# A causal convolution of 31 taps: the first 12 taps of two of its four channel tiles go to ScalarE and GpSimd

## The chip, the core and the metric

The kernel runs on one core of a Trainium2 chip. The time is that of the whole kernel on the device, in microseconds (us), as a median of several runs; lower is better. One further execution was taken with the hardware profiler, and all rows below are from it. Engines are named as the profile does: PE (TensorE), DVE (VectorE), ACT (ScalarE), POOL (GpSimd), SP (SyncE). "L1546" is line 1546 of the kernel before.

## The reference, cut to what matters

Two transformer blocks run over 256 tokens of width 1024. The second one starts with a mixer that has a convolution and a retention half. Only the convolution is touched:

```
def conv_module(a, b, conv_w, conv_b, ln_w, ln_b):
    u = a * jax.nn.sigmoid(b)
    y = lax.conv_general_dilated(
        u, conv_w[:, None, :], window_strides=(1,), padding=[(CONV_WIDTH - 1, 0)],
        dimension_numbers=("NWC", "WIO", "NWC"), feature_group_count=CONV_CH) + conv_b
    yf = y.astype(jnp.float32)
    mu = jnp.mean(yf, axis=-1, keepdims=True)
    var = jnp.mean(jnp.square(yf - mu), axis=-1, keepdims=True)
    yn = (yf - mu) * lax.rsqrt(var + EPS) * ln_w + ln_b
    return jax.nn.silu(yn)
```

CONV_WIDTH is 31 and CONV_CH is 512, so each of 512 channels is filtered by its own 31 weights along the tokens. With channels on the partitions that is 4 tiles of 128 channels x 256 tokens with 31 taps each: 124 multiply-adds of a whole 128x256 tile.

## The kernel before, in words

Each weight matrix streams through a ring of four buffers, `raw`. SP starts the load of a chunk (128x1024 for the phases here) when the chunk four before it has been used up, ACT rounds it to `whi` (split_hi, L365), DVE subtracts to get the rest, `wlo` (split_lo, L376), and PE multiplies with both (L398 to L400, 24 matmuls to a strip). The five engines run programs of their own, each in the order written, and meet only at semaphores.

The stage around the change is `mixb`, with the phase `memk` behind it: 28 steps q = 0 to 27, one weight chunk each, from about 582 to 685 us of the span. Steps 0 to 7 give the four tiles of the gated input `glu`, steps 8 to 11 the queries and keys `qr` that are rotated at once, 12 to 15 the values, 16 to 19 a gate, and 20 to 27 the keys of a memory attention, whose results ACT copies to `km[:, 0]` to `km[:, 7]`. PE, ACT and DVE each have one function that loops over q (pe_mixb, act_mixb, dve_mixb). In a step DVE reads a result out of a bank (L1632), does its share of the rotation (steps 10 to 13, tile e = q - 10: L1569, L1570 and L1572) or of the retention (from step 13, RET0), then split_lo, and then a number of convolution taps: conv_taps, from step 4 (TAP0), as many as the list in taps_before says. A tap is one multiply-add of a 128x256 tile of `glu`, shifted by j tokens, onto `cy` (L1546; the first of a tile, with the bias, is L1542). Tiles 0 and 1 are done first, in turns, then tiles 2 and 3. After step 26 the sums for the layer norm of the convolution follow (dve_layer_norm, from L1590).

PE depends on DVE and ACT at these places, apart from `wlo`: the rotation matmul of tile e at step 9 + e (L1357) needs, for e = 2 and 3, that DVE has read out the one two tiles earlier (L1570, through `rot_step`); the spread of `m_inv` at step 15 (L420) needs DVE's reciprocal of step 14 (L1575); the transposes of the values (L1366, four of them at steps 13 to 16) need ACT's two scaled copies of the one before (L1464, through `rv_copied`); the retention's second product (L1413, at steps 15, 17, 19, 21) needs DVE's masked scores `amat` (L1647) and, from the second on, ACT's root (L1520, through `gn_sd`).

ACT's step is, in order: split_hi, one scaled tile of `mem` (L1452, steps 10 to 17), sigmoids, the scaled copies L1464 (steps 14 to 17), roots and copies of the retention (L1520, L1527 and L1528), and last the copy of the step's bank (act_mixb_copy, L1492; steps 8 to 15 and 20 to 27). POOL has little to do: it computes the rotary angles of the positions near the start of the kernel (L2095 to L2108), fills masks, and in this stage starts loads: `mem_rows`, `mem` and, at steps 5 to 12, four pieces of `decay` (L2143). DVE needs piece u at step 14 + 2u.

Of the kernel before, what the change touches and what calls it, by code (L numbers as in the profile page):

```python
# [26 lines left out]
ALU = mybir.AluOpType  # L27
ACT = mybir.ActivationFunctionType
# [6 lines left out]
NX = 256  # L35
# [8 lines left out]
HEADS = 8  # L44
# [6 lines left out]
TAPS = 31  # L51
# [47 lines left out]
def build(nc, io):  # L99
# [12 lines left out]
    with ctx:  # L112
        def sem(name):
            return ctx.enter_context(nc.semaphore(name))
# [29 lines left out]
        vecs = place("vecs", [P, V_COLS])  # L144
        convw = place("convw", [P, 4 * TAPS])
# [143 lines left out]
        decay_in, mem_in, glu_zero = sem("decay_in"), sem("mem_in"), sem("glu_zero")  # L289
        cs_act, cs_dve = sem("cs_act"), sem("cs_dve")  # L290
        cb_sig, glu_done, conv_step = sem("cb_sig"), sem("glu_done"), sem("conv_step")
        rot_mm, rot_step, rg_done = sem("rot_mm"), sem("rot_step"), sem("rg_done")
        m_scaled, m_hi, m_lo, m_sq, rows_in, m_sd, m_inv, m_bc, m_r = (
            sem(s) for s in ("m_scaled", "m_hi", "m_lo", "m_sq", "rows_in", "m_sd", "m_inv", "m_bc", "m_r"))
# [1015 lines left out]
        sc, sgrp = first["mixb"]  # L1310
        STEPS = counts["mixb"] + counts["memk"]
        TAP0 = 4
        RET0 = 13
        ROWS0, MEM0 = 4, 10
        LN0 = 27

        def taps_before(q):

            steps = [4] * 6 + [3] * 4 + [5] * 3 + [8] * 3 + [7] * 7
            return min(sum(steps[:q - TAP0]), 4 * TAPS)  # L1320

        assert taps_before(LN0) == 4 * TAPS
        RV = 12

        def pe_mixb(pe):
# [106 lines left out]
        def act_mixb(act):  # L1432
            for q in range(STEPS):
                if q < 20:
                    split_hi(act, sc, 1, q, LEAD)
                if q == 0:
                    act_norm(act, N_MIXB, False)
                if q == 1:

                    act.wait_ge(angle_step, ANGLE_STEPS)  # L1440
                    nc.scalar.activation(sinv[:, :], angle[:, :], ACT.Sin).then_inc(cs_act, 1)
                    nc.scalar.activation(cosv[:, :], angle[:, :], ACT.Sin, scale=0.5).then_inc(cs_act, 1)
                if q in (ROWS0, ROWS0 + 1):
                    b = q - ROWS0
                    act.wait_ge(rows_in, 16)
                    nc.scalar.activation(vmem[:, b, :], vmem[:, b, :], ACT.Square,
                                         accum_out=msum[:, b:b + 1]).then_inc(m_sq, 1)
                if MEM0 <= q < MEM0 + KT:
                    e = q - MEM0
                    if e == 0:  # L1450
                        act.wait_ge(mem_in, 16)
                    nc.scalar.activation(mem[:, e, :], mem[:, e, :], ACT.Copy, scale=gain(N_MEM, e)).then_inc(m_scaled, 1)  # L1452
                if q < 8 and q % 2 == 0:
                    act.wait_ge(acc_free, sgrp + q + 1)
                    nc.scalar.activation(sg[:, 0:NX], tg[:, 0:NX], ACT.Sigmoid).then_inc(cb_sig, 1)
                if q == 13:
                    act.wait_ge(m_sq, 2)
                    nc.scalar.activation(col_root[:, 0, 0:2], msum[:, :], ACT.Sqrt, bias=epsc[:, 0:1],
                                         scale=1.0 / D).then_inc(m_sd, 1)
                if RV + 2 <= q < RV + 6:  # L1460
                    t = q - 2 - RV
                    act.wait_ge(rv_tr, t + 1)
                    for b in range(2):
                        nc.scalar.activation(v2[:, b, t * P:(t + 1) * P], ps[3][:, NX + b * P:NX + (b + 1) * P],  # L1464
                                             ACT.Copy, scale=inv[:, b:b + 1]).then_inc(rv_copied, 1)
                if q == 15:
                    act.wait_ge(m_bc, 1)
                    nc.scalar.activation(memr[:, :], ps[7][:, 0:NX], ACT.Copy).then_inc(m_r, 1)
                if 17 <= q < 21:
                    act.wait_ge(acc_free, sgrp + q)  # L1470
                    src = tg if q % 2 else tu
                    nc.scalar.activation(rg[:, q - 17, :], src[:, 0:NX], ACT.Silu).then_inc(rg_done, 1)
                if q >= RET0:
                    act_retention(act, q - RET0)
                act_layer_norm(act, q - LN0)
                if 8 <= q < RV:
                    act_mixb_copy(act, q, qr[:, q - 8, :])
                if RV <= q < RV + 4:
                    if q == RV + 1:
                        act.wait_ge(glu_done, 4)  # L1480
                    if q >= RV + 2:
                        act.wait_ge(rv_tr, q - RV - 1)
                    act_mixb_copy(act, q, (tu if q % 2 else tg)[:, 0:NX])
                if q >= 20:
                    act_mixb_copy(act, q, km[:, q - 20, :])
                    split_hi(act, sc, 1, q, LEAD)

        def act_mixb_copy(act, q, dst):

            act.wait_ge(pe_done, sc + q + 1)  # L1490
            act.wait_ge(acc_free, sgrp + q)
            nc.scalar.activation(dst, ps[banks[sgrp + q]][:, 0:NX], ACT.Copy).then_inc(acc_free, 1)  # L1492

        def act_layer_norm(act, step):
            if step == 1:
# [37 lines left out]

        def conv_taps(dve, a, b):

            for n in range(a, min(b, 4 * TAPS)):
                t, j = n // (2 * TAPS) * 2 + n % 2, n % (2 * TAPS) // 2
                src = glu[:, t, j:j + NX]
                w = convw[:, t * TAPS + j:t * TAPS + j + 1]
                if j == 0:  # L1540
                    dve.wait_ge(glu_done, t + 1)
                    nc.vector.tensor_scalar(cy[:, t, :], src, w, vecs[:, V_CONVB + t:V_CONVB + t + 1], ALU.mult,  # L1542
                                            ALU.add).then_inc(conv_step, 1)
                else:
                    dve.wait_ge(conv_step, n - 1)
                    nc.vector.scalar_tensor_tensor(cy[:, t, :], src, w, cy[:, t, :], ALU.mult, ALU.add).then_inc(conv_step, 1)  # L1546
# [39 lines left out]
        def dve_layer_norm(dve, step):  # L1586
            if step == -1:

                dve.wait_ge(conv_step, 4 * TAPS)
                nc.vector.tensor_tensor(csq[:, 0:2, :], cy[:, 0:2, :], cy[:, 2:4, :], ALU.add).then_inc(ln_sum, 1)  # L1590
                dve.wait_ge(ln_sum, 1)
                nc.vector.tensor_tensor(csq[:, 0, :], csq[:, 0, :], csq[:, 1, :], ALU.add).then_inc(ln_sum, 1)
            if step == 1:
                dve.wait_ge(ln_mu, 1)
                for t in (0, 2):
                    nc.vector.scalar_tensor_tensor(cy[:, t:t + 2, :],
                                                   ps[4][:, 0:NX].unsqueeze(1).to_broadcast([P, 2, NX]), -1.0 / CONV,
                                                   cy[:, t:t + 2, :], ALU.mult, ALU.add).then_inc(ln_cen, 1)
            if step == 2:
                dve.wait_ge(ln_sq, 2)  # L1600
                nc.vector.tensor_tensor(csq[:, 0:2, :], csq[:, 0:2, :], csq[:, 2:4, :], ALU.add).then_inc(ln_sum, 1)
                dve.wait_ge(ln_sum, 3)
                nc.vector.tensor_tensor(csq[:, 0, :], csq[:, 0, :], csq[:, 1, :], ALU.add).then_inc(ln_sum, 1)
            if step == 3:
                dve.wait_ge(ln_sd, 1)
                nc.vector.reciprocal(csq[:, 1, :], csq[:, 1, :]).then_inc(ln_r, 1)
            if step == 4:
                dve.wait_ge(ln_r, 1)
                for t in range(4):
                    nc.vector.scalar_tensor_tensor(cy[:, t, :], cy[:, t, :], vecs[:, V_LNW + t:V_LNW + t + 1],  # L1610
                                                   csq[:, 1, :], ALU.mult, ALU.mult).then_inc(ln_n, 1)
                for t in range(4):
                    dve.wait_ge(c_hi, t + 1)
                    nc.vector.tensor_tensor(oz2[:, 4 + t, 1, :], cy[:, t, :], oz2[:, 4 + t, 0, :],
                                            ALU.subtract).then_inc(c_lo, 1)
# [456 lines left out]
        def _(pool):  # L2072
# [63 lines left out]
            pool.dma_start(vmem[:, :, :], io["mem_rows"]).then_inc(rows_in, 16)  # L2136
            pool.wait_ge(pe_done, sc + 3)
            pool.dma_start(mem[:, :, :], io["mem"]).then_inc(mem_in, 16)
            for u in range(HEADS // 2):
                pool.wait_ge(pe_done, sc + 6 + 2 * u)  # L2140
                if u:
                    pool.wait_ge(decay_in, 16 * u)
                pool.dma_start(decay[:, 2 * u:2 * u + 2, :], io["decay"][:, 2 * u:2 * u + 2, :]).then_inc(decay_in, 16)  # L2143

        @block.scalar
        def _(act):
# [243 lines left out]
```

## Time and profile before

| | before |
|---|---|
| median of 3 runs | 985.16 us (984.95 to 985.96) |
| the profiled execution, its own time | 985.93 us |
| its span, first to last instruction | 984.1 us |
| PE busy | 969.7 us, 99% |
| DVE busy | 693.9 us, 71% |
| ACT busy | 513.3 us, 52% |
| POOL busy | 37.4 us, 4% |
| mean granted clock of PE, share of full speed | 0.997 |

Shares of busy time are averages over the whole span. In a timeline row the first number is the start in us, the second how long the instruction or the run of xN instructions lasted; instructions overlap at their ends, so the rate of an engine is read from start to start. In brackets stands how long the engine was idle before it and what ended that.

### The profile page before, as it was taken

What the parts mean: (1) busy time and instruction counts of PE and PEld (TensorE: products, weight loads), DVE (VectorE), ACT (ScalarE), POOL (GpSimd) and SP (SyncE); (2) the same over time, 40 slices, a digit from 0 to 9 for tenths busy, and PEclk for the clock granted to TensorE, in tenths of its full rate; (3) what the DMA queues carried; (4) which work ended last, traced back from release to release, by engine and by line L of the source; (5) the groups of instructions that cost most, each with busy time, mean ns of one, the idle gap of its engine ahead of it and who ended that gap; (6) DMA issues with size and microseconds to landing.
All of it is one profiled execution on the core that took longest, in us unless ns stands there. A gap on an engine that the chain in (4) does not pass through costs nothing.

```text
span 984.1 us, 19828 instructions
## 1 busy us (share of the span) xinstructions
PE 969.7 (99%) x7333; PEld 919.7 (93%) x7333; DVE 693.9 (71%) x1231; ACT 513.3 (52%) x825; POOL 37.4 (4%) x59
## 2 busy tenths in 40 slices
PE   8999999999999999999999999999999999999997
PEld 7999999999988898999998899888998999998886
DVE  6866675556688778866676559999885398885553
ACT  6544454455465665655454447642765465444441
POOL 4600000001000000000000000000000000000000
PEclk9999999999999999999999999999999999999998
DMA  7555566546633355655566557514545346555551
GB/s 265 193 170 174 176 224 207 185 129 177 182 117 113 103 171 172 194 190 182 183 221 209 180 177 250 180 65 150 193 150 173 128 152 204 185 188 191 186 189 53
DMA packets 46188, 170.61 MB, mean 173 GB/s; under 512 B 5512, under 2 KB 6304, under 8 KB 45872
## 3 DMA queue, kind: packets, MB, share of 16 engines
q1 hardware_dynamic: 44352, 163.20, 50.4%
q0 software_dynamic: 1632, 6.56, 2.3%
q8 instruction: 40, 0.66, 0.3%
q14 instruction: 20, 0.16, 0.1%
q10 hardware_dynamic: 144, 0.03, 0.0%
HBM read 168.71 MB, written 1.06 MB: 173 GB/s over the span
## 4 chain that ended last, share of the span: by engine, by line
PE 89%; DVE 6%; ACT 2%; DMA 1%; issue 1%; SPq 0%; DVEq 0%
PE bank L398 20%; PE bank L399 20%; PE bank L400 20%; PE bank L402 11%; PE bank L403 6%; PE bank L1340 3%; DVE wlo L376 2%; DVE cy L1546 1%; PE bank L1787 1%; PE bank L1788 1%; PE bank L1789 1%; PE bank L1862 1%; PE bank L1887 1%; DMA res<-in_res 1%; PE bank L947 1%
## 5 line engine op out<-in xcount | busy, mean ns | idle before, releaser
L398 PE MATMUL bank<-x,whi 128*128 128x256 f32 (+1 forms) x1464 | 418.2, 286 | 3.0 <-DVE x L505 2.5
L399 PE MATMUL bank<-x,whi 128*128 128x256 f32 (+1 forms) x1464 | 414.2, 283 | 0.0
L400 PE MATMUL bank<-x,wlo 128*128 128x256 f32 (+1 forms) x1464 | 413.3, 282 | 0.0
L376 DVE TENSOR_TENSOR wlo<-raw,whi 128x1024 fp32r<-128x1024 f32 (+1 forms) x285 | 360.0, 1266 | 39.2 <-ACT whi L365 39.1
L365 ACT ACTIVATE whi<-raw 128x1024 fp32r<-128x1024 f32 (+1 forms) x285 | 309.0, 1087 | 95.1 <-PE bank L400 42.5
L398 PEld LDWEIGHTS bank<-x,whi 128*128 128x128 f32 x1464 | 275.3, 188 | 11.4 <-issue 3.8
L400 PEld LDWEIGHTS bank<-x,wlo 128*128 128x128 f32 x1464 | 275.7, 188 | 0.0
L399 PEld LDWEIGHTS bank<-x,whi 128*128 128x128 f32 x1464 | 275.0, 188 | 0.3
L402 PE MATMUL bank<-hid,whi 128*128 128x512 f32 x400 | 141.4, 396 | 0.0
L403 PE MATMUL bank<-hid,wlo 128*128 128x256 f32 x400 | 112.8, 282 | 0.0
L402 PEld LDWEIGHTS bank<-hid,whi 128*128 128x128 f32 x400 | 75.2, 188 | 18.0
L403 PEld LDWEIGHTS bank<-hid,wlo 128*128 128x128 f32 x400 | 75.1, 188 | 0.0
L485 ACT ACTIVATE x<-res,gains 128x256 fp32r<-128x256 f32 (+2 forms) x48 | 24.2, 510 | 75.8 <-DVE res L780 38.9
L654 ACT ACTIVATE hid<-hd 128x272 f32 (+3 forms) x44 | 18.7, 424 | 86.3 <-DVE hd L689 86.3
L398 PE MATMUL bank<-hid,whi 128*128 128x272 f32 (+1 forms) x208 | 59.6, 286 | 0.0
L400 PE MATMUL bank<-hid,wlo 128*128 128x272 f32 (+1 forms) x208 | 59.4, 286 | 0.0
L399 PE MATMUL bank<-hid,whi 128*128 128x272 f32 (+1 forms) x208 | 59.4, 286 | 0.0
L1546 DVE SCALAR_TENSOR_TENSOR cy<-glu,convw,cy 128x256 f32<-128x256 f32 x120 | 49.5, 480 | 0.0
L777 DVE SCALAR_TENSOR_TENSOR res<-bank,res 128x256 f32<-128x256 f32 (+1 forms) x23 | 9.7, 423 | 50.2 <-PE bank L403 50.2
L686 DVE TENSOR_TENSOR tu<-bank,rstd 128x272 f32<-128x272 f32 (+1 forms) x44 | 19.0, 432 | 36.6 <-PE bank L400 36.6
L682 DVE TENSOR_TENSOR tg<-bank,rstd 128x272 f32<-128x272 f32 (+1 forms) x44 | 19.0, 432 | 28.9 <-PE bank L400 28.9
L399 PEld LDWEIGHTS bank<-hid,whi 128*128 128x128 f32 x208 | 39.3, 189 | 0.0
(280 smaller groups left out, 1207.4 us busy)
## 6 DMA issues: line engine op xcount, KB each, us to landing
raw<-in_w_f2in SPq DMA_DIRECT2D x44, 512.0 KB, 3.4
raw<-in_w_f1in SPq DMA_DIRECT2D x42, 512.0 KB, 3.5
raw<-in_w_mix SPq DMA_DIRECT2D x35, 512.0 KB, 3.7
raw<-in_w_up SPq DMA_DIRECT2D x32, 512.0 KB, 4.2
raw<-in_w_down SPq DMA_DIRECT2D x32, 512.0 KB, 4.3
raw<-in_w_f1out SPq DMA_DIRECT2D x16, 704.0 KB, 4.2
raw<-in_w_f2out SPq DMA_DIRECT2D x16, 704.0 KB, 4.2
raw<-in_w_mixb SPq DMA_DIRECT2D x20, 512.0 KB, 3.5
```

What stands on the lines that cost most here:

```text
L365: nc.scalar.activation(whi[:, s, 0:tiles * P], raw[:, s, 0:tiles * P], ACT.Copy).then_inc(w_hi, 1)
L376: nc.vector.tensor_tensor(wlo[:, s, 0:tiles * P], raw[:, s, 0:tiles * P], whi[:, s, 0:tiles * P], ALU.subtract).then_inc(w_lo, 1)
L398: nc.tensor.matmul(out, whi[:, s, w], hi, start=first, stop=False)
L399: nc.tensor.matmul(out, whi[:, s, w], lo, start=False, stop=False)
L400: mm = nc.tensor.matmul(out, wlo[:, s, w], hi, start=False, stop=last)
L402: nc.tensor.matmul(out, whi[:, s, w], both, start=first, stop=False)
L403: mm = nc.tensor.matmul(out[:, 0:NX], wlo[:, s, w], hi, start=False, stop=last)
L485: nc.scalar.activation(x_tile(0, m, full), res_tile(m, full), ACT.Copy, scale=gain(n, m)).then_inc(x_hi, 1)
L682: nc.vector.tensor_tensor(tg[:, 0:width], out, rstd[:, 0:width], ALU.mult).then_inc(acc_free, 1)
L686: nc.vector.tensor_tensor(tu[:, 0:width], out, rstd[:, 0:width], ALU.mult).then_inc(acc_free, 1)
L1340: mm = nc.tensor.matmul(out[:, 0:NX], raw[:, s, t * P:(t + 1) * P], mem[:, t, :], start=t == 0, stop=t == KT - 1)
L1546: nc.vector.scalar_tensor_tensor(cy[:, t, :], src, w, cy[:, t, :], ALU.mult, ALU.add).then_inc(conv_step, 1)
```

## The change

Tiles 2 and 3 get their first 12 taps from two other engines. At steps 8 to 19, ACT multiplies `glu`, shifted by j = q - 8, with the tap's weight, for tile 2 and for tile 3 (act_taps). The products of j = 0, with the bias, go to `cy` itself; the 22 others go to four spare buffers, `km[:, 4]` to `km[:, 7]`, which are not used for the keys before step 24. POOL adds each of the 22 onto `cy`. ACT may be four products ahead of POOL at most: from j = 3 on it waits for `pool_step`. Act_taps stands behind the copy of the bank at steps 8 to 11, and ahead of it at steps 12 to 15. POOL's later loads of `decay` are set between the adds: piece 1 ahead of the third add, 2 and 3 six adds later each.

DVE does 100 taps in place of 124. Its list over the steps is new: 3 in place of 4 at steps 4 to 9, 2 in place of 3 at 10 to 13, 4 in place of 5 at 14 to 16, 6 in place of 8 at 17 to 19, 6 in place of 7 at 20 to 24, and 7 as before at 25 and 26. At its first tap of tile 2 and of tile 3 it waits for POOL's last add of that tile, which comes at step 21.

```diff
         TAP0 = 4
+        POOL_TAPS = 12
+        DVE_TAPS = 4 * TAPS - 2 * POOL_TAPS
 ...
-            steps = [4] * 6 + [3] * 4 + [5] * 3 + [8] * 3 + [7] * 7
-            return min(sum(steps[:q - TAP0]), 4 * TAPS)
+            steps = [3] * 6 + [2] * 4 + [4] * 3 + [6] * 8 + [7] * 2
+            return min(sum(steps[:q - TAP0]), DVE_TAPS)
 ...
                 if 8 <= q < RV:
                     act_mixb_copy(act, q, qr[:, q - 8, :])
+                if 8 <= q < 8 + POOL_TAPS:
+                    act_taps(act, q - 8)
                 if RV <= q < RV + 4:
 ...
+                if q == 24:
+                    act.wait_ge(pool_step, 2 * POOL_TAPS - 2)
 ...
+        def act_taps(act, j):
+
+            for t in (2, 3):
+                n = 2 * j + t - 2
+                src = glu[:, t, j:j + NX]
+                w = convw[:, t * TAPS + j:t * TAPS + j + 1]
+                if j == 0:
+                    if t == 2:
+                        act.wait_ge(const_in, 80)
+                        act.wait_ge(glu_zero, 1)
+                    act.wait_ge(glu_done, t + 1)
+                    nc.scalar.activation(cy[:, t, :], src, ACT.Identity, scale=w,
+                                         bias=vecs[:, V_CONVB + t:V_CONVB + t + 1]).then_inc(tap_prod, 1)
+                else:
+                    if n >= 6:
+                        act.wait_ge(pool_step, n - 5)
+                    nc.scalar.activation(km[:, 4 + n % 4, :], src, ACT.Copy, scale=w).then_inc(tap_prod, 1)
 ...
-            for n in range(a, min(b, 4 * TAPS)):
-                t, j = n // (2 * TAPS) * 2 + n % 2, n % (2 * TAPS) // 2
+            for n in range(a, min(b, DVE_TAPS)):
+                t, j = (n % 2, n // 2) if n < 2 * TAPS else (2 + n % 2, n // 2 - TAPS + POOL_TAPS)
 ...
+                if t >= 2 and j == POOL_TAPS:
+                    dve.wait_ge(pool_step, 2 * POOL_TAPS - 4 + t - 1)
 ...
-                dve.wait_ge(conv_step, 4 * TAPS)
+                dve.wait_ge(conv_step, DVE_TAPS)
 ...
-            for u in range(HEADS // 2):
+
+            def load_decay(u):
                 pool.wait_ge(pe_done, sc + 6 + 2 * u)
 ...
+            load_decay(0)
+            for n in range(2, 2 * POOL_TAPS):
+                if n in (4, 10, 16):
+                    load_decay((n + 2) // 6)
+                t = 2 + n % 2
+                pool.wait_ge(tap_prod, n + 1)
+                if n >= 4:
+                    pool.wait_ge(pool_step, n - 3)
+                nc.gpsimd.tensor_tensor(cy[:, t, :], cy[:, t, :], km[:, 4 + n % 4, :], ALU.add).then_inc(pool_step, 1)
```

## Rows read from the trace of the kernel before

**Rows 1.** The page's first part: busy us, share of the span, instructions.

```profile
PE 969.7 (99%) x7333; PEld 919.7 (93%) x7333; DVE 693.9 (71%) x1231; ACT 513.3 (52%) x825; POOL 37.4 (4%) x59
```

**Rows 2.** Waits of PE from 570 to 740 us: total, times, longest.

```profile
PE bank L1357 <- DVE hd L1570: 1.1, 1, 1.1
PE bank L1695 <- DVE oz L1614: 1.0, 1, 1.0
PE bank L1381 <- DVE csq L1603: 0.6, 1, 0.6
```

**Rows 3.** Busy time by windows: PE, PEld, DVE, ACT, POOL, clock, DMA share, GB/s.

```profile
610.00:620.00 10.00, 8.95 (x71) 8.61 (x70) 9.97 (x21) 5.44 (x10) 1.07 (x2) 1.00 0.69 229
```

**Rows 4.** Timeline of PE at steps 11, 12, 15, 16 and 17.

```profile
618.23 0.67 PE L1357 MATMUL bank<-qr,swap 128*128 128x256 f32 x2 [1.05 <-DVE hd L1570]
...
621.68 0.67 PE L1357 MATMUL bank<-qr,swap 128*128 128x256 f32 x2
...
633.38 0.87 PE L1413 MATMUL bank<-amat,v 128*64 128x256 f32 x8
...
636.99 0.28 PE L400 MATMUL bank<-x,wlo 128*128 128x256 f32 x1
637.22 0.68 PE L1366 MATMUL bank<-center,tu 128*128 128x128 f32 x4
...
642.16 0.87 PE L1413 MATMUL bank<-amat,v 128*64 128x256 f32 x8
```

**Rows 5.** Timeline of DVE at steps 9, 10, 11 and 14.

```profile
615.74 1.68 DVE L1546 SCALAR_TENSOR_TENSOR cy<-glu,convw,cy 128x256 f32<-128x256 f32 x4
617.32 0.43 DVE L1569 TENSOR_TENSOR qr<-qr,cosv 128x256 f32<-128x256 f32 x1
617.66 0.43 DVE L1570 TENSOR_TENSOR hd<-bank,sinv 128x256 f32<-128x256 f32 x1
...
621.12 0.42 DVE L1570 TENSOR_TENSOR hd<-bank,sinv 128x256 f32<-128x256 f32 x1
...
631.22 1.00 DVE L1647 TENSOR_TENSOR amat<-bank,decay 128x384 f32<-128x384 f32 x2
```

**Rows 6.** Timeline of ACT at steps 9, 16, 17 and 19.

```profile
610.70 0.38 ACT L1492 ACTIVATE qr<-bank 128x256 f32<-128x256 f32 x1 [0.55 <-PE bank L400]
...
636.05 0.52 ACT L1452 ACTIVATE mem<-mem,gains 128x256 f32<-128x256 f32 x1
636.45 0.63 ACT L1464 ACTIVATE v<-bank,inv 128x128 f32<-128x128 f32 x2
...
641.61 0.26 ACT L1520 ACTIVATE col_root<-bank,epsc 128x4 f32<-128x4 f32 x1
...
651.90 0.38 ACT L1527 ACTIVATE msq<-bank 128x256 f32<-128x256 f32 x1 [2.94 <-PE bank L1413]
```

**Rows 7.** Timeline of POOL: angles near the start, one load of the stage.

```profile
23.75 0.74 POOL L2107 TENSOR_TENSOR angle<-angle,part 128x256 f32<-128x256 f32 x1
...
35.85 0.93 POOL L2106 TENSOR_SCALAR part<-turns 128x256 f32<-128x256 f32 x1
36.86 1.14 POOL L2107 TENSOR_TENSOR angle<-angle,part 128x256 f32<-128x256 f32 x1
...
617.47 0.54 POOL L2143 DMA_DIRECT2D decay<-in_decay  x1 [5.98 <-PE bank L400]
```

**Rows 8.** Timeline of DVE beside POOL's angles.

```profile
24.18 1.39 DVE L376 TENSOR_TENSOR wlo<-raw,whi 128x1024 fp32r<-128x1024 f32 x1 [0.51 <-ACT whi L365]
...
35.62 0.44 DVE L689 TENSOR_TENSOR hd<-tu,sg 128x272 f32<-128x272 f32 x1
35.99 1.41 DVE L376 TENSOR_TENSOR wlo<-raw,whi 128x1024 fp32r<-128x1024 f32 x1
...
38.74 1.22 DVE L376 TENSOR_TENSOR wlo<-raw,whi 128x1024 fp32r<-128x1024 f32 x1
```

More of the change, by code:

```diff
@@ L291, in build @@
         cb_sig, glu_done, conv_step = sem("cb_sig"), sem("glu_done"), sem("conv_step")
+        tap_prod, pool_step = sem("tap_prod"), sem("pool_step")
         rot_mm, rot_step, rg_done = sem("rot_mm"), sem("rot_step"), sem("rg_done")
@@ L1317, in taps_before @@
         def taps_before(q):
-            steps = [4] * 6 + [3] * 4 + [5] * 3 + [8] * 3 + [7] * 7
-            return min(sum(steps[:q - TAP0]), 4 * TAPS)
-        assert taps_before(LN0) == 4 * TAPS
+            steps = [3] * 6 + [2] * 4 + [4] * 3 + [6] * 8 + [7] * 2
+            return min(sum(steps[:q - TAP0]), DVE_TAPS)
+        assert taps_before(LN0) == DVE_TAPS
         RV = 12
```

## The prediction, made before the changed kernel was run

> **What bounds the kernel now.** I read the views from the whole to the place. The page's busy times come first: PE is at work for 99% of the span, DVE for 71% [rows 1]. So a DVE that does less work brings nothing by itself; only time in which PE stands still for DVE can be won. Second, PE's waits around the stage: three of note, 1.05 us at the rotation matmul L1357, and 0.6 and 1.0 us in the layer norm behind the stage [rows 2]. The latter two hang on a chain (sums, centring, squares, root) that starts after the last tap and that the change leaves alone. That caps the gain: about 1.05 us of 985, 0.11%. Third, the windows: in the stretch of the first wait DVE is busy 9.97 of 10 us [rows 3], so it was late because its queue was full. Fourth, the timelines, to see which of PE's other needs are met only just. They carry the sum, because moved work can make new waits there.
>
> **What is removed.** DVE loses 24 of 124 taps. Four taps take from 615.74 to 617.32, that is 0.395 us each [rows 5]; in all 9.5 us of DVE work. By step 10 six are gone, 2.37 us.
>
> **What is added on ACT.** 24 products of 128x256 with a scale column. Their nearest row is the `mem` product, from 636.05 to the next start at 636.45: 0.40 us each [rows 6], so 0.80 per step. Where ACT was waiting for PE anyway they cost nothing. The first pair uses Identity with a bias, which no row shows; between nothing and two loads of a function table it falls in steps 8 and 9, where PE is three strips behind ACT's splits, and I put it at nothing. Queued behind each pair are the bank copy and the next split_hi, for which DVE and SP wait in turn.
>
> **What is added on POOL.** 22 adds of 128x256. The same kind of instruction stands in the angles: 0.74 us undisturbed, 1.14 us disturbed [rows 7]. The disturbance can be read: DVE's weight split is 1.22 us alone, but 1.39 when it starts within POOL's add of 23.75, as if it got going at 24.35; and POOL's add of 36.86 ends 0.67 us after the split that began at 35.99 lets go (35.99 + 1.41, less the usual overlap of 0.08) [rows 7, 8]. So a POOL add and a DVE operation with both inputs in SBUF don't run side by side here: one waits, and the add holds the other off for up to 0.60 us. Taps have both inputs in SBUF, as have the splits and two of three rotation steps. Who wins when DVE's instructions follow without a gap? POOL asked at 35.85, in the middle of DVE's 35.62 to 36.06, and was done at 36.78, while DVE's next, at 35.99, came out at 1.41 in place of 1.22 [rows 7, 8]: POOL went in between. So I expect POOL to wait for one DVE instruction at most (0.4 to 1.14 us) and DVE to be pushed back by each add. The bounds are 0 (it falls beside PSUM reads) and 0.60 us; I take 0.50, since of DVE's step of 3.46 us (617.66 to 621.12 [rows 5]) only one operation of 0.4 reads PSUM. Twenty-two adds then cost DVE 11 us, against 9.5 us of taps taken off. DVE is relieved of nothing; work is only shifted, away from steps 4 to 8, into steps 9 to 19.
>
> The Trainium skill has this as a rule ("SBUF — State Buffer", section "SBUF: two separate sides"): VectorE operations with two SBUF inputs and GpSimd operations that read SBUF take turns on one port pair, held for the whole instruction. The rows agree on who blocks whom, but show a hold of 0.60, not the whole 0.74 us. By the whole of it 22 adds would cost DVE 16.3 us, and the time would come out at the upper end below.
>
> POOL itself: 1.3 us to an add, with the wait, is 2.6 us a step, and the loads of `decay` add 0.54 us each [rows 7], three in 11 steps. PE takes 3.45 us for step 12 (618.23 to 621.68) and 8.8 for the two from 633.38 to 642.16 [rows 4]. POOL keeps up, so neither ACT's wait for `pool_step` nor DVE's at step 21 bites. The loads of `decay` go out later than now (617.47 for the last one, some 20 us later then) but DVE needs them only at step 14 + 2u.
>
> **The sum along PE's path.** A shift is against before.
> - Steps 4 to 10: DVE's L1570 of tile 0 ends at 618.09 [rows 5]. Minus 2.37, plus some 3.5 adds by then (those of j = 1, and most of j = 2) at 0.50, 1.75: shift -0.62, end 617.47. PE follows 0.14 us behind, as it does now (618.09 to 618.23), at 617.61; it could have come at 618.23 - 1.05 = 617.18 [rows 4]. Won 0.62.
> - Step 11: one tap less (-0.395), two adds (+1.0): L1570 of tile 1, now from 621.12 to 621.54, shifts by -0.62 + 0.60 = -0.02. PE's L1357 at 621.68 comes exactly 0.14 us behind it already [rows 4, 5]. So it can't move before DVE does: the 0.62 us are given back, shift 0.
> - Steps 11 to 14: three taps less (-1.19), 5.5 adds (+2.75): DVE is 1.54 us late at `amat`, which ends at 632.22; PE's L1413 wants it at 633.38, room 1.02 with the 0.14 taken off [rows 4, 5]. The reciprocal L1575 just ahead of it has as much room or more. New wait 0.52.
> - Steps 15 and 16: from PE's L1413 of 633.38 ACT goes through square, copy, bank copy, split, `mem` (636.05), and the two scaled copies of 636.45, which end at 637.08; PE's L1366 starts at 637.22, again 0.14 behind, though its strip let go at 636.99 + 0.12 = 637.11 [rows 4, 6]. PE is waiting for ACT here already, by 0.1. The pair of j = 7 is queued in this chain, between the square's copy and the bank copy, and nothing in it has slack: +0.80.
> - Step 17: the pair of j = 8 makes ACT's root at 641.61 about 0.4 us later beside L1366 (half of it hides in L1366's own run), with room of 642.16 - 641.87 - 0.14 = 0.15 [rows 4, 6], if PE's delay is counted: 0.1 to 0.2. I take 0.1.
> - From step 18 I see no wait: the last pair comes behind ACT's square and copy of 651.90 [rows 6], so at about 652.5 to 653.3, and its adds are in by about 656, a step ahead of DVE's need, and DVE has a tap less in steps 20 to 24. The layer norm's start follows PE's strips as now: nothing.
> In sum 0 + 0.52 + 0.80 + 0.1 = +1.4 us. All later waits are counted from PE, so it stays to the end. The profiled execution had a span of 984.1 and a time of 985.93, 0.77 above the median; the shift is put on the median: 985.16 + 1.4 = 986.6.
>
> **The rivals.**
> - The adds cost DVE next to nothing. DVE's shifts are then all negative: all 1.05 us won at step 11, nothing lost at 14, but ACT's 0.9 us stay: -0.15, 985.0. For it: PSUM reads and DVE's own semaphore gaps. Against: both disturbed splits of rows 8. Chance 0.20.
> - Neither that nor the ACT chain costs anything, because ACT's products run earlier than I place them: -1.05, 984.1. Against: the order is written out, and ACT's copy and PE's L1366 are 0.14 us apart. Chance 0.08. No case gives more than that, so a gain over 0.2% has hardly a source.
> - POOL falls behind (the slower side). If it gets its turn only when DVE reads PSUM or waits, not after each instruction, an add takes far longer. ACT, four products ahead at most, then stands, and with it splits and copies. Place and point: the first add can start when ACT has copied (610.70) and made one product, 611.4; the last pair, due at 652.5, needs 18 adds and three loads of 0.54 before it [rows 6, 7]. So it decides from (652.5 - 611.4 - 1.6) / 18 = 2.2 us per add. At 2.6 us the last pair may start at 611.4 + 46.8 + 1.6 = 659.8: +7.3, 992.5. For it: at steps 10 to 13 DVE runs without a gap [rows 3]. Against: the turn of 35.85. Chance 0.08.
> - The change doesn't do what it says: the first pair brings table loads, or DVE doesn't catch up in steps 4 to 9. Within 1 us of the forecast; chance 0.04.
>
> **How the numbers follow.** My case has 0.60. Its own range is from one add fewer at each place (+0.9) to the whole hold of 0.60 us with four, two and six adds: shifts +0.03, +0.84, +3.25, so a new wait of 2.2 in place of 0.52, and +3.1 in sum, 988.3. The 8-in-10 range takes in the first rival and part of the second: 984.4 to 988.6. A measurement here can't tell less than about 0.2%, 1.97 us: the borders are 983.2 and 987.1. Slower: a quarter of my case (0.15) and the third rival (0.08), 0.23. Faster: 0.03. The same: 0.74.
>
> **What would show it.** In the profile after: PE's wait at L1357 of e = 2 down to some 0.4 us and a new one of about 0.6 at e = 3; PE waiting for DVE's reciprocal or `amat` at step 15 by 0.5; PE waiting for ACT's scaled copies at step 16 by 0.9; POOL's adds at 0.7 to 1.8 us; DVE taps of up to 1.0 us in steps 9 to 19 and of 0.48 before and after. I am wrong if taps keep 0.395 us while POOL adds, if PE's wait at step 16 stays at 0.1, or if ACT waits for `pool_step`.

## The result and the profile after

| | before | after |
|---|---|---|
| median, 8 runs each | 985.76 us (984.95 to 987.38) | 988.22 us (987.27 to 990.59) |
| ratio to before, 95% interval | | 1.0026 (1.0015 to 1.0037) |
| the profiled execution: span | 984.1 us | 988.7 us |
| the stage's stretch (below) | 100.44 us | 101.96 us |

The changed kernel is slower by 0.26%, 2.5 us, just over the 0.2% below which the forecast calls two times the same; the interval starts below it. 986.6 was forecast, with 984.4 to 988.6 as the range.

The two profiled executions differ by 1.94 us at the entry of the stage already, in stages with the same work. So spans aren't compared; the measure from here on is one stretch inside each profile, from PE's sums of squares in step 0 to its first sum of the layer norm. Its two ends in the kernel before, from PE's timeline:

```profile
584.39 0.28 PE L413 MATMUL bank<-ones,sqsum 128*128 128x1 f32 x2
...
684.83 0.70 PE L1378 MATMUL bank<-csq,ones 128*128 128x256 f32 x2
```

and in the kernel after (its lines are 1 to 28 higher than before's; L1381 is the first layer norm sum):

```profile
586.33 0.28 PE L414 MATMUL bank<-ones,sqsum 128*128 128x1 f32 x2
...
688.29 0.48 PE L1381 MATMUL bank<-csq,ones 128*128 128x256 f32 x1
```

684.83 - 584.39 = 100.44, and 688.29 - 586.33 = 101.96: the stage is 1.52 us longer. The same stretch was 100.44 and 100.44 in two executions of the kernel before, 101.96 and 101.95 in two of the kernel after, so it can be read to a few hundredths. The page's busy times, against [rows 1]:

```profile
PE 974.0 (99%) x7333; PEld 923.8 (93%) x7333; DVE 692.4 (70%) x1207; ACT 522.8 (53%) x849; POOL 56.5 (6%) x81
```

DVE has 24 instructions fewer, and is nearly as busy as it was: 692.4 us against 693.9. By its 24 taps it should have 9.5 us less. Waits of PE in the stage, in total, times and longest, against [rows 2] ("bank" is a bank of PSUM, the memory that PE writes its results to; L1360 is the rotation matmul, L1597 DVE's read-out for it, L1369 the transposes of the values, L1467 ACT's scaled copies):

```profile
PE bank L1360 <- DVE hd L1597: 1.7, 2, 1.1
PE bank L1722 <- DVE oz L1641: 1.0, 1, 1.0
PE bank L1369 <- ACT v L1467: 0.8, 1, 0.8
PE bank L1384 <- DVE csq L1630: 0.6, 1, 0.6
```

Where there was one wait of 1.05 us at a rotation matmul, there are two, of 0.62 and 1.06 together 1.7, and there is one more, for ACT. The two in the layer norm are what they were. A wait costs PE somewhat more than its row says. The idle time is counted from the end of the last matmul, 0.28 us after its start, and matmuls that follow without a wait start 0.12 us apart: a wait of 1.05 us is worth about 1.2 from start to start. PE's timeline, against [rows 4]:

```profile
619.73 0.67 PE L1360 MATMUL bank<-qr,swap 128*128 128x256 f32 x2 [0.62 <-DVE hd L1597]
...
624.29 0.67 PE L1360 MATMUL bank<-qr,swap 128*128 128x256 f32 x2 [1.06 <-DVE hd L1597]
...
640.61 0.68 PE L1369 MATMUL bank<-center,tu 128*128 128x128 f32 x4 [0.75 <-ACT v L1467]
```

DVE's timeline at steps 8 to 13 (L1573 are taps, L377 the weight split, L1596, L1597 and L1599 the rotation), against [rows 5]:

```profile
611.05 1.27 DVE L1573 SCALAR_TENSOR_TENSOR cy<-glu,convw,cy 128x256 f32<-128x256 f32 x3
...
613.38 2.24 DVE L1573 SCALAR_TENSOR_TENSOR cy<-glu,convw,cy 128x256 f32<-128x256 f32 x3
...
616.68 2.24 DVE L1573 SCALAR_TENSOR_TENSOR cy<-glu,convw,cy 128x256 f32<-128x256 f32 x3
618.84 0.41 DVE L1596 TENSOR_TENSOR qr<-qr,cosv 128x256 f32<-128x256 f32 x1
619.17 0.41 DVE L1597 TENSOR_TENSOR hd<-bank,sinv 128x256 f32<-128x256 f32 x1
...
621.10 1.84 DVE L1573 SCALAR_TENSOR_TENSOR cy<-glu,convw,cy 128x256 f32<-128x256 f32 x2
622.86 0.95 DVE L1596 TENSOR_TENSOR qr<-qr,cosv 128x256 f32<-128x256 f32 x1
623.73 0.41 DVE L1597 TENSOR_TENSOR hd<-bank,sinv 128x256 f32<-128x256 f32 x1
...
628.02 1.75 DVE L377 TENSOR_TENSOR wlo<-raw,whi 128x1024 fp32r<-128x1024 f32 x1
```

Three taps take 1.27 us where POOL is idle and 2.24 where it adds twice: 0.97 for two adds, 0.49 each. One product of the rotation takes 0.95 in place of 0.41, one split 1.75 in place of 1.22. The read-out L1597, with one input in PSUM, stays at 0.41, at 623.73 too, where POOL is adding. POOL at the same time:

```profile
613.50 1.83 POOL L2181 TENSOR_TENSOR cy<-cy,km 128x256 f32<-128x256 f32 x2 [11.37 <-ACT km L1517]
615.28 0.56 POOL L2171 DMA_DIRECT2D decay<-in_decay  x1
616.77 1.86 POOL L2181 TENSOR_TENSOR cy<-cy,km 128x256 f32<-128x256 f32 x2 [0.93 <-ACT km L1517]
620.01 4.39 POOL L2181 TENSOR_TENSOR cy<-cy,km 128x256 f32<-128x256 f32 x4 [1.38 <-ACT km L1517]
```

Ahead of each of these runs of adds POOL waits for ACT's products, not the other way round, and ACT never waits for POOL. The run of four from 620.01 is the pair of step 11 and that of step 12 without a pause: act_taps stands behind the bank copy at step 11, and ahead of it at step 12, so the two come 2.2 us apart on ACT. Last, ACT at steps 15 and 16 (L1553 the copy beside the square, L1517 the products, L1499 the bank copy), against [rows 6]:

```profile
637.17 0.38 ACT L1553 ACTIVATE csq<-bank 128x256 f32<-128x256 f32 x1
637.43 0.91 ACT L1517 ACTIVATE km<-glu,convw 128x256 f32<-128x256 f32 x2
638.23 0.38 ACT L1499 ACTIVATE tu<-bank 128x256 f32<-128x256 f32 x1
638.50 1.07 ACT L366 ACTIVATE whi<-raw 128x1024 fp32r<-128x1024 f32 x1
639.44 0.51 ACT L1455 ACTIVATE mem<-mem,gains 128x256 f32<-128x256 f32 x1
639.84 0.63 ACT L1467 ACTIVATE v<-bank,inv 128x128 f32<-128x128 f32 x2
```

The pair takes from 637.43 to 638.23, 0.80 us, everything behind it in the chain follows at once, and PE's L1369 starts at 640.61, 0.14 behind the end of L1467.

### The profile page after: what moved, and what is told of

Its sections match the earlier page's. It is cut to its first block, busy times and chain, and to the rows that moved or that the text cites. A ratio compares the mean times of both kernels' runs of the same rounds, so it can differ in the third digit from the quotient of the medians.

```text
span 988.7 us, 19873 instructions
## 1 busy us (share of the span) xinstructions
PE 974.0 (99%) x7333; PEld 923.8 (93%) x7333; DVE 692.4 (70%) x1207; ACT 522.8 (53%) x849; POOL 56.5 (6%) x81
## 3 DMA queue, kind: packets, MB, share of 16 engines
HBM read 168.71 MB, written 1.06 MB: 172 GB/s over the span
## 4 chain that ended last, share of the span: by engine, by line
PE 88%; DVE 7%; ACT 2%; issue 1%; DMA 1%; SPq 0%; DVEq 0%; ACTq 0%
PE bank L399 20%; PE bank L400 19%; PE bank L401 19%; PE bank L403 11%; PE bank L404 6%; PE bank L1343 2%; DVE wlo L377 2%; DVE cy L1573 1%; PE bank L1814 1%; PE bank L1815 1%; PE bank L1816 1%; ACT whi L366 1%; PE bank L1914 1%; PE bank L1889 1%; PE bank L948 1%
## 5 line engine op out<-in xcount | busy, mean ns | idle before, releaser
L377 DVE TENSOR_TENSOR wlo<-raw,whi 128x1024 fp32r<-128x1024 f32 (+1 forms) x285 | 360.7, 1269 | 39.2 <-ACT whi L366 39.1
L1573 DVE SCALAR_TENSOR_TENSOR cy<-glu,convw,cy 128x256 f32<-128x256 f32 x98 | 45.8, 529 | 0.0
```

The source lines that it names most:

```text
L377: nc.vector.tensor_tensor(wlo[:, s, 0:tiles * P], raw[:, s, 0:tiles * P], whi[:, s, 0:tiles * P], ALU.subtract).then_inc(w_lo, 1)
```

## The experiments

The theory: the stage is longer by 1.5 us for two reasons. DVE is pushed back by POOL's turns in steps 9 to 12, where it has no time to spare; and ACT's pair of step 15 lies in a chain that PE waits for. The rivals: DVE is late for its new list of taps or a wait on POOL, ACT is late in general, or there is a third cost. All stretches and ratios:

| kernel | stretch, us | ratio to before (95%) |
|---|---|---|
| before, twice | 100.44, 100.44 | second: 1.0010 (0.9997 to 1.0023) |
| after, twice | 101.96, 101.95 | 1.0026 (1.0015 to 1.0037), 1.0021 (1.0010 to 1.0032) |
| respread, twice | 99.26, 99.25 | 0.9995 (0.9985 to 1.0006), 0.9982 (0.9971 to 0.9993) |
| moved | 101.13 | 1.0011 (1.0001 to 1.0021) |
| both, twice | 99.30, 99.27 | 0.9993 (0.9984 to 1.0002), 0.9986 (0.9974 to 0.9997) |
| noadd | 99.97 | 1.0002 (0.9989 to 1.0014) |
| noadd_moved | 99.12 | 0.9981 (0.9971 to 0.9991) |
| late12 | 101.98 | 1.0020 (1.0009 to 1.0031) |
| late12_moved | 101.87 | 1.0007 (0.9995 to 1.0020) |
| addsonly | 107.82 | 1.0058 (1.0043 to 1.0073) |

**noadd: POOL's adds without their reads.** In the kernel after:

```diff
-nc.gpsimd.tensor_tensor(cy[:, t, :], cy[:, t, :], km[:, 4 + n % 4, :], ALU.add).then_inc(pool_step, 1)
+nc.gpsimd.memset(km[:, 4 + n % 4, 0:8], 0.0).then_inc(pool_step, 1)
```

> The changed kernel, with POOL's 22 adds replaced by a fill of 8 columns of the product buffer just used, with the same waits and signals: POOL reads nothing from SBUF, and the products of taps 1 to 11 are left out of tiles 2 and 3. Theory (the adds push DVE back, by about 0.5 us each): taps 0.395 us apart throughout, both waits at the rotation matmuls gone, the ACT wait of 0.75 at step 16 stays, stretch 100.44 - 1.05 + 0.8 + 0.1 = 100.2 to 100.3. Rival (DVE is late because of its new list or of waits on POOL, not because of the adds' SBUF reads): stretch 101.9.

The stretch was 99.97, somewhat below the 100.2 expected: the missing wait of 1.05 is worth 1.2, as said above. DVE's taps are back at 1.27 for three, at steps 8 and 9 and ahead of the first rotation read-out, and both rotation waits are gone:

```profile
610.31 1.27 DVE L1573 SCALAR_TENSOR_TENSOR cy<-glu,convw,cy 128x256 f32<-128x256 f32 x3
611.50 1.22 DVE L377 TENSOR_TENSOR wlo<-raw,whi 128x1024 fp32r<-128x1024 f32 x1
612.63 1.27 DVE L1573 SCALAR_TENSOR_TENSOR cy<-glu,convw,cy 128x256 f32<-128x256 f32 x3
```

```profile
PE bank L1722 <- DVE oz L1641: 0.8, 1, 0.8
PE bank L1369 <- ACT v L1467: 0.8, 1, 0.8
PE bank L1384 <- DVE csq L1630: 0.6, 1, 0.6
```

The list and the order of waits are as in the kernel after; only the adds differ. They cost 101.96 - 99.97 = 1.99 us of the stretch, all that the relief of DVE had won and more. DVE is busy for 685.3 us here, so over the whole kernel the 24 taps were worth 8.6 us of its busy time and the 22 adds took back 7.1 (692.4 - 685.3), 0.32 each on average. The wait for ACT stayed, as the second cost should.

**moved: the pairs of steps 15 and 16 elsewhere.** One goes ahead of ACT's wait for PE's spread in step 15, the other behind the root in step 17:

```diff
-                if 8 <= q < 8 + POOL_TAPS:
+                if 8 <= q < 8 + POOL_TAPS and q not in (15, 16):
 ...
                 if q == 15:
+                    act_taps(act, 7)
                     act.wait_ge(m_bc, 1)
 ...
                                      scale=1.0 / HD).then_inc(gn_sd, 1)
+                if r == 4:
+                    act_taps(act, 8)
```

> The changed kernel, with two of ACT's twelve pairs of products at other places in ACT's order: the pair of step 15 ahead of ACT's wait for the spread means (2.2 us idle), the pair of step 16 behind ACT's root of step 17 (1.2 us idle). Theory (the pair of step 15 lies in a chain PE waits for, and costs its own length): PE's wait for ACT's scaled copies at step 16 goes from 0.75 to about 0, stretch 101.96 - 0.87 = 101.1. Rival (that wait comes from ACT being late in general, or POOL then falls behind): stretch 101.7 to 102.

The stretch was 101.13, 0.83 less, and the wait for L1467 was gone. So it was not ACT's load, but where a few instructions stood. Both pairs were moved in one run, which can't divide the 0.83 between them; the shifts of PE in the kernel after do, with 0.80 at step 16 and 0.07 at step 17 (the table further down). The 20 other products weren't touched, and PE waits for none of them.

**noadd_moved: both edits.** 

> The changed kernel with both of its costs taken out: the two pairs of ACT moved out of the chain PE waits for, and POOL's adds replaced by fills of 8 columns (the products of taps 1 to 11 are left out of tiles 2 and 3). Theory (these two are all): no wait of PE from step 11 to step 17, stretch 99.97 - 0.80 = 99.2, what the mere new spread of DVE's taps reached (99.26). Rival (a third cost): 99.6 or more.

99.12: waits of PE between steps 11 and 17 are gone, and there is no third cost in the stage. Against before this is -1.32. Of it -1.22 is there at the rotation matmul of step 11 already, which is the wait of 1.05 us [rows 2] from start to start; in "respread", below, the same place gives -1.18.

**respread: DVE's list alone, on the kernel before.**

```diff
-            steps = [4] * 6 + [3] * 4 + [5] * 3 + [8] * 3 + [7] * 7
+            steps = [4] * 3 + [3] * 7 + [5] * 3 + [8] * 6 + [7] * 4
```

> The kernel before, with nothing changed but DVE's list of taps: one tap fewer at each of steps 7 to 9, made up at steps 20 to 22. All 124 taps stay on DVE. The stretch from PE's sums at the start of the stage to the first sum of the layer norm is 100.44 us before and 101.96 after. Theory (PE's only wait here is there because DVE's queue is too full by step 10): the wait of 1.05 us at the second-last rotation matmul goes, stretch 99.4, ratio to before 0.999. Rival (the wait is set by something else than the number of taps, or DVE's delay comes back at steps 20 to 22): stretch 100.4 or more, ratio 1.000.

99.26: three of 124 taps moved to later steps take away the whole wait and give nearly as much as 24 taps taken off DVE at no price (99.12). DVE was not short of time in the stage as a whole, only ahead of step 10.

**both: the moved pairs, and five taps of DVE later.** In the kernel "moved":

```diff
-            steps = [3] * 6 + [2] * 4 + [4] * 3 + [6] * 8 + [7] * 2
+            steps = [2] * 5 + [3] + [2] * 4 + [4] * 3 + [7] * 5 + [6] * 3 + [7] * 2
```

> As the kernel with the two moved pairs, and DVE does five taps fewer at steps 4 to 9 (2,2,2,2,2,3 in place of 3 each), made up at steps 17 to 21. Theory (all of the change's cost is the ACT chain and DVE's delay through POOL's turns at steps 9 to 12, and DVE has time to spare from step 17 on): no wait of PE between steps 11 and 17, stretch 99.4 to 99.6, 1 us below before, ratio to before 0.999. Rival (DVE's delay through POOL's turns is too large or comes elsewhere): stretch 100.4 or more.

99.30, without a wait of PE from step 11 to 17. So the change can be mended. But it then stands where the kernel before gets with a new list alone (99.26): ACT's products and POOL's adds bring nothing on top.

**late12: the pair of step 12 behind the bank copy.** In the kernel after, to pull the run of four adds apart:

```diff
-                if 8 <= q < 8 + POOL_TAPS:
+                if 8 <= q < 8 + POOL_TAPS and q != 12:
 ...
                     act_mixb_copy(act, q, (tu if q % 2 else tg)[:, 0:NX])
+                if q == 12:
+                    act_taps(act, 4)
```

> The changed kernel, with ACT's pair of products of step 12 behind the copy of that step's bank, not ahead of it, so that POOL's two adds for it come later. Theory (the second rotation wait of 1.06 us is as long as it is because that pair lets POOL take four turns in a row, of which three or four fall before the read-out PE waits for): this wait falls to 0.1 to 0.6 us, DVE's rotation product of tile 1 loses its 0.54 us of delay, and the stretch falls from 101.96 to 101.1 to 101.5. Rival (each step has its two adds in any case and only the sum of turns counts): stretch 101.9.

The wait at the second rotation matmul fell from 1.06 to 0.53, as expected, and DVE's rotation product to 0.41, but the stretch stayed at 101.98: the rival's number. What is left of this wait is put down to ACT's bank copy, which ends 0.03 us behind DVE's read-out. The gain was given back by step 17: PE is late against before by 0.15 us at step 12, 0.46 at step 15, 1.26 at step 16 and 1.55 at step 17.

**late12_moved: to see where it went.** The edits of "late12" and "moved" together. 

> The kernel in which the pair of step 12 comes behind the bank copy gained 0.53 us at PE's second rotation wait and lost it again by step 17, to waits for ACT. Here the pairs of steps 15 and 16 are moved out of ACT's chain as well. Theory (what was lost went to that chain): no wait for ACT's scaled copies at step 16, stretch 101.13 (the moved pairs alone) - 0.5 = 100.6. Rival (the gain of step 12 goes to DVE's own lateness at step 14): 101.1.

101.87, worse than "moved" alone, 101.13, and outside what either side expected. The wait at L1369 is gone, but there is a new one at step 15, for DVE's reciprocal:

```profile
PE bank L421 <- DVE col_inv L1607: 0.8, 1, 0.8
PE bank L1360 <- DVE hd L1602: 0.6, 1, 0.6
PE bank L1360 <- ACT tg L1502: 0.5, 1, 0.5
```

It stands where the forecast had put one. DVE's timeline ahead of the reciprocal, and POOL's beside it:

```profile
632.82 1.83 DVE L1578 SCALAR_TENSOR_TENSOR cy<-glu,convw,cy 128x256 f32<-128x256 f32 x2
634.57 0.15 DVE L1607 RECIPROCAL col_inv<-col_root 128x2 f32<-128x2 f32 x1
```

```profile
632.68 1.68 POOL L2186 TENSOR_TENSOR cy<-cy,km 128x256 f32<-128x256 f32 x2 [1.21 <-ACT km L1520]
```

Counted from the start of the stretch, the reciprocal begins at 47.83 us in the kernel after, at 48.32 in "late12" and at 49.29 here. The first 0.49 comes with the adds taken away from step 12, which are still made some 2 us later. The other 0.97 comes with the pair of step 15: "moved" has ACT make it ahead of its wait for the spread, and its two adds now fall on DVE's two taps of step 14, 1.83 us in place of 0.87. In "moved" alone the same two adds came as these taps ended, beside the reciprocal and the masked scores, and cost 0.24 us. As long as DVE has no time to spare, moving adds between steps changes where the lateness shows, not that it is there; "both" got rid of it by moving DVE's own taps past step 16.

**addsonly: the price of the turns alone.** The kernel before, with all taps on DVE and none on ACT, and POOL adding between scratch tiles:

```diff
 ...
+            nc.gpsimd.memset(km[:, 4:8, :], 0.0).then_inc(pool_step, 1)
 ...
+            for n in range(2, 24):
+                if n in (4, 10, 16):
+                    load_decay((n + 2) // 6)
+                pool.wait_ge(pe_done, sc + 9 + n // 2)
+                pool.wait_ge(pool_step, max(n - 2, 1))
+                nc.gpsimd.tensor_tensor(km[:, 4 + n % 2, :], km[:, 4 + n % 2, :], km[:, 6 + n % 2, :], ALU.add).then_inc(pool_step, 1)
```

> The kernel before with all its 124 taps on DVE and no products on ACT, and 22 adds of 128x256 on POOL between four scratch tiles, two per step of PE from step 10 to 20: the price of POOL's turns by itself. Theory (an add puts DVE off by 0.49 us, the taps 2.24 us for three in the changed kernel against 1.27 before): DVE, which has no time to spare up to step 20 and some 2.1 us after it, is 10.7 us late, and PE waits at the rotation matmuls and for the masked scores: stretch 100.44 + 8.6 = 109, between 107 and 110. Rival (POOL's adds fall mostly beside operations that don't mind, so that the changed kernel's delay is a matter of a few collisions): stretch 101 to 103.

107.82, 7.4 us longer. The whole time is longer too, by a ratio of 1.0058, which is 5.7 us (4.2 to 7.2, of four executions); why that is less than the stretch isn't shown. Its waits of PE:

```profile
PE bank L1358 <- DVE hd L1573: 4.0, 1, 4.0
PE bank L1414 <- ACT col_root L1523: 1.9, 2, 1.0
```

Before its first rotation wait there are six adds: 1.05 + 6 x 0.49 = 3.99, and 3.97 was read. So an add of POOL's is a delay of 0.49 us for a DVE whose operations each read two operands from SBUF and follow without a gap. Were all 22 to fall like that, they would take 10.8 us, more than the 9.5 of the 24 taps; in the changed kernel they took the 7.1 read above.

The 7.4 us are not the price of the turns alone. PE's timeline behind the wait, and its busy time with the granted clock, the figure 0.50, in the 5.5 us from there:

```profile
621.54 1.19 PE L1358 MATMUL bank<-qr,swap 128*128 128x256 f32 x2 [3.97 <-DVE hd L1573]
```

```profile
621.50:627.00 5.50, 5.46 (x23) 5.31 (x24) 5.46 (x11) 0.00 (x0) 0.00 (x0) 0.50 0.31 98
```

PE had stood still for 3.97 us, and then ran at the lower of its two levels, 1.2 GHz, with a matmul each 0.21 us in place of 0.12. From this rotation matmul to the next it took 5.91 us, where the kernel before takes 3.45 [rows 4]. So the 7.4 us are 2.95 of a longer wait at the first of them, some 2.4 of slow clock, and 2.0 at two later waits for ACT's root (L1414), the first of which comes behind a wait of ACT for DVE of 1.20 us. The theory's 8.6 had only DVE's lateness in it; that the number came out in its range of 107 to 110 bears out the delay per add, but not that sum. In the other runs no wait of PE in the stage was longer than 1.07 us, and its granted clock stayed at 1.00.

**The kernels run again.** 

> The changed kernel once more, word for word. Its first timing gave 988.22 against 985.76 us, 2.5 us, while its stage grew by 1.52 us in the profile. Theory (the stage is all there is; the rest of the difference varies from one execution to the next with PE's rate in other stages): stretch from PE's sums to the first sum of the layer norm again 101.9 to 102.0, ratio to before near 1.0015. Rival (the change also slows something outside of the stage): ratio again 1.0025 or more, and the profile longer by the same amount in the same later stage as the first time.

> The kernel before, word for word. In its first profile PE's matmuls of the last MLP's up stage (720 to 880 us) started every 0.1167 us, in the changed kernel's two profiles every 0.1178, which makes 0.9 us over that stage. Theory (the change doesn't reach that stage, and the rate is drawn anew in each execution): either rate here. Rival (it belongs to the kernel, for some reason of its code): 0.1167 again. The stretch from PE's sums to the first sum of the layer norm is 100.44 again; ratio 1.000.

> The kernel with the two moved pairs and the new spread of DVE's taps, word for word; its stretch was 99.30, its rate in the up stage 0.1167, its ratio 0.9993 (0.9984 to 1.0002). Theory: stretch 99.3, ratio 0.9985 to 0.9993. If the rate belongs to the kernel it is 0.1167 again.

> The kernel before with only DVE's list changed, word for word; its stretch was 99.26, its rate in the up stage 0.1178, its ratio 0.9995. Theory: stretch 99.3, ratio 0.9985 to 0.9997. If the rate belongs to the kernel it is 0.1178 again; if it is drawn per execution, it may be 0.1167.

The stretches came back to 0.03 us or better. This leaves the difference between the stretch (+1.52 us, 0.15%) and the medians (0.26% and 0.21%, 2.5 and 2.1 us). Some of it lies in the up stage of the last MLP. Busy time from 830 to 860 us, with PE's matmuls in the first bracket, for before, after, "both" and "respread", in this order:

```profile
830.00:860.00 30.00, 30.00 (x260) 30.00 (x259) 24.78 (x44) 15.39 (x22) 0.00 (x0) 1.00 0.57 188
```

```profile
830.00:860.00 30.00, 30.00 (x257) 30.00 (x256) 24.56 (x43) 14.39 (x22) 0.00 (x0) 1.00 0.58 185
```

```profile
830.00:860.00 30.00, 30.00 (x260) 30.00 (x259) 24.71 (x45) 14.60 (x22) 0.00 (x0) 1.00 0.58 184
```

```profile
830.00:860.00 30.00, 30.00 (x257) 30.00 (x256) 24.59 (x43) 14.29 (x22) 0.00 (x0) 1.00 0.56 184
```

PE is never idle and its granted clock is 1.00 in all, but 260 matmuls fall into these 30 us in one and 257 in the other. These counts include the two or three that had begun before; from start to start it is one each 0.1167 or 0.1178 us, some 0.9 us over the 846 matmuls of this stage. In the second execution of each of the four the count was 259, 257, 260 and 257. The six other kernels fall on the same two rates: "moved", "noadd", "late12" and "addsonly" on 0.1178, "noadd_moved" and "late12_moved" on 0.1167. So the rate seems to go with the kernel, against what I had expected, and the kernel after has the longer of the two. Stretch and rate together are 1.5 + 0.9 = 2.4 us, beside 2.5 and 2.1 measured. It is no cost of the change in any useful sense: "respread", which only reorders DVE's work in the convolution's stage, has 0.1178 too, and "both", with all of the change's adds, 0.1167. What sets it is open, and four kernels profiled twice are few: four pairs alike would come by chance once in 16 times, if the two rates were drawn evenly.

## Why the prediction was right, and where its steps were off

The time lay in the range, on the side that was forecast, at +2.5 us where +1.4 was said. The chance given to "slower by over 0.2%" was 0.23, and the measured 0.26% is that case by its middle; the interval includes 0.2%. Shifts of PE against before, counted from the start of the stretch:

| place | forecast | measured |
|---|---|---|
| rotation matmul of step 11 | -0.62 | -0.44 |
| rotation matmul of step 12 | 0 | +0.67 |
| first L1413, step 15 | +0.52 | +0.65 |
| L1366 of step 16 | +1.32 | +1.45 |
| second L1413, step 17 | +1.42 | +1.52 |
| layer norm's first sum | +1.42 | +1.52 |

- The cap was right in kind: the one wait was all that could be had from DVE's relief. Its 1.05 us are worth 1.2 from start to start, and the best kernels won 1.1 to 1.3 of stretch.
- The turns on SBUF were right, in who blocks whom and in size: 0.50 per add taken, 0.49 measured. Read from two disturbed splits of the angles [rows 7, 8], it carried the sum. Some of the match is luck: 0.50 was chosen below a hold of 0.60 because a part of DVE's operations read PSUM, but 0.49 is what an add costs a DVE that reads none. The 11 us for all 22 were too much; DVE's busy time shows 7.1, so "DVE is relieved of nothing" holds up to step 14 and not for the whole, where 1.5 us were left. "Four adds before step 10's read-out" (3.5 taken) explains -0.44 in place of -0.62.
- The step that was off is the term of step 11: two adds were put there, +1.0, but the order of act_taps and bank copy brings step 12's pair forward, and three fall ahead of the read-out. DVE's tap pair and rotation product take 0.97 and 0.54 more, 1.5 in all. PE's shift came out +0.67 in place of 0.
- The term of steps 11 to 14 was 0.52 of new wait, and nothing was to be seen there: PE was already late by 0.67, which widened the room of 1.02 to 1.69, and DVE was 1.07 late at `amat` (634.23 - 1.94 against 631.22), not 1.54. With ten taps less, 3.96 us, that is 5.0 us of adds: about ten of them, where 11 were forecast. So the two errors are mostly one delay that showed at another place. That the sum of the stage came within 0.1 us of the forecast, +1.52 against +1.42, with one step 0.67 off and the next 0.5, is partly luck.
- ACT's chain was forecast at +0.80 and measured at +0.80 (from +0.65 to +1.45); "moved" took it away. Step 17 gave +0.07, 0.1 forecast.
- The first rival (adds cost DVE nothing, 985.0) fell to the taps of 2.24 us, to "noadd" and to the first wait of "addsonly"; the second (ACT's pair costs nothing) to "moved". The third, POOL falling behind, did not come: an add took 0.98 us on average of 22, less than half of the 2.2 from which it would decide, and ACT never waited for `pool_step`. That POOL gets its turn between two of DVE's back-to-back instructions, read from one place near 36 us, held for all. Identity loaded no table.
- Missing from the sum: 0.9 us in the up stage, a stage that I hadn't looked at. Most of the distance from +1.4 to +2.5 is this, and its cause is open.

The rule of the Trainium skill on the shared port pair ("SBUF — State Buffer", section "SBUF: two separate sides") held here in what it excludes: DVE operations with one input in PSUM ran on beside adds at 0.41 us. Its "whole instruction" is too long for the price, and the measurement decides: the delay was 0.49 us, and POOL's shortest add in the rows 0.74.

## What to carry to other kernels

Work taken off DVE and given to POOL is mostly not off DVE, if both read two operands from SBUF: here one add of POOL cost a full DVE 0.49 us, and the tap it replaced 0.40; over the whole kernel 8.6 us were taken off and 7.1 came back. If PE waits for an engine that is full only for some steps, first move work along the steps; three taps of 124, moved by a list, won nearly all there was. And for each instruction put into a busy engine's order, look for the chain it stands in: of ACT's 24 products all but a few were free, and one pair, put between PE's result and what PE waits for next, cost 0.8 us. Last, look at PE's granted clock behind a long wait before its cost is put down to the wait: in "addsonly" 2.4 of 7.4 us were the clock's.

## What the runs showed of the hardware that I had not expected

PE's rate in a stage that no one waits in differs by 1% (0.1167 or 0.1178 us per matmul of 256 columns, at a granted clock of 1.00) between kernels whose code for PE is the same, and came back the same in the second execution of each of four kernels; ten kernels showed these two rates and no third. It is worth 0.9 us here, as much as the effects under study. A stretch that ends before that stage is free of it, a whole time is not.
